# Moving the second tile's delta rule behind the first tile's expert choices, with fewer row buffers and panel slots lent twice

## The reference, cut to what matters

```python
h = _rmsnorm(x, norm1); proj = h @ w_in                    # split into 12 parts
o_a = _gated_delta_rule(q, k, v, beta, log_alpha)           # "delta": 64-token chunks in the reference
o_b = _hgrn2_recurrence(qb, 1 - f_gate, ib, log(f_gate))    # "hgrn"
mix = sigmoid(g_a) * (o_a @ w_branch_a) + sigmoid(g_b) * (o_b @ w_branch_b)
x = x + mix @ w_out
h2 = _rmsnorm(x, norm2)
# product keys: for 8 heads the top 16 of 128 x 128 keys, so 128 experts a token
s = einsum(h2 @ w_pq, sub_keys); idx, gate = top16(...)
y[t] = sum_k gate[t,k] * gelu(h2[t] . expert_u[idx[t,k]]) * expert_v[idx[t,k]]
```

## Time and profile before

| | us |
|---|---|
| median of 3 runs (1853.99 to 1854.33) | 1854.06 |
| the profiled execution, its own time | 1848.71 |
| its span, first to last instruction | 1846.9 |
| PE busy | 1614.6 (87%) |
| DVE busy | 993.5 (54%) |
| ACT busy | 461.3 (25%) |
| gathers, packets of queue q0 | 268.45 MB, 35.2% of 16 engines' span |
| HBM read | 469.04 MB, 255 GB/s over the span |

### The profile page before, as it was taken

One profiled execution on the slowest core, in us unless ns is written; L12 is line 12 of the kernel. 1 busy time (PEld: TensorE's weight loads), 2 busy tenths in 40 slices (PEclk: granted clock), 3 DMA queues, 4 the chain that ended last, 5 costly groups with the idle time before them and its releaser, 6 DMA issues.

```text
span 1846.9 us, 19442 instructions
## 1 busy us (share of the span) xinstructions
PE 1614.6 (87%) x7700; PEld 1076.7 (58%) x7700; DVE 993.5 (54%) x1843; ACT 461.3 (25%) x1018; POOL 312.2 (17%) x269
## 2 busy tenths in 40 slices
PE   7999989999897996989877667668999999899997
PEld 6857656764845553346423222227997486489963
DVE  3433334331676786358996666653666415356654
ACT  1152152240243554123323322221000013310001
POOL 0000000000112443233545545520000000000000
PEclk9999989999998998999988998899999999999999
DMA  6444221125799799999999999993644443155433
GB/s 243 175 157 168 86 92 46 48 101 209 315 424 369 311 422 419 425 422 419 421 420 421 422 421 421 422 392 126 223 166 154 183 160 137 46 205 183 174 146 114
DMA packets 55192, 471.32 MB, mean 255 GB/s; under 512 B 6592, under 2 KB 7744, under 8 KB 10432
## 3 DMA queue, kind: packets, MB, share of 16 engines
q0 software_dynamic: 36864, 268.45, 35.2%
q1 hardware_dynamic: 18240, 201.66, 28.8%
HBM read 469.04 MB, written 1.05 MB: 255 GB/s over the span
## 4 chain that ended last, share of the span: by engine, by line
PE 63%; DMA 17%; DVE 11%; ACT 4%; issue 3%; POOL 1%; SPq 0%; DVEq 0%; ACTq 0%; POOLq 0%
PE ps L2385 13%; DMA main<-in_expert_uv,main 10%; PE ps L489 7%; PE ps L445 6%; PE ps L1014 5%; PE ps L2542 5%; PE ps L415 5%; DMA panels<-in_expert_uv,main 4%; PE ps L1252 4%; DVE main L942 3%; PE ps L2312 3%; PE ps L2331 2%; PE ps L1486 2%; PE ps L485 2%; PE ps L2308 2%
## 5 line engine op out<-in xcount | busy, mean ns | idle before, releaser
L1014 PE MATMUL ps<-main 128*128 128x512 f32 x680 | 339.2, 648 | 95.6 <-ACT main L989 95.2
L924 POOL DMA_INDIRECT main<-in_expert_uv,main x208 | 246.8, 1187 | 377.5 <-PE ps L1014 225.7
L942 DVE SCALAR_TENSOR_TENSOR main<-main 128x1024 f32<-128x1024 f32 x208 | 249.5, 1223 | 93.2 <-DMA main<-in_expert_uv,main 92.0
L1014 PEld LDWEIGHTS ps<-main 128*128 128x128 f32 x680 | 134.5, 206 | 279.6 <-issue 145.9
L1014 PE MATMUL ps<-panels,main 128*128 128x512 f32 x148 | 81.7, 699 | 44.9 <-ACT main L989 37.2
L977 ACT ACTIVATE main<-main 128x2 f32<-128x2 f32 x128 | 25.9, 202 | 364.2 <-DVE main L942 299.2
L445 PE MATMUL ps<-panels,xT 128*128 128x512 f32 x256 | 112.5, 592 | 0.0
L2385 PE MATMUL ps<-main 128*128 128x128 f32 x912 | 104.9, 275 | 0.0
L2385 PEld LDWEIGHTS ps<-main 128*128 128x128 f32 x912 | 103.4, 192 | 0.0
L489 PE MATMUL ps<-panels,main 128*128 128x512 f32 x192 | 87.4, 615 | 4.9 <-ACT main L547 4.9
L1252 PEld LDWEIGHTS ps<-main 128*128 128x128 f32 x704 | 82.0, 192 | 11.9 <-issue 8.8
(11 more groups left out here) (320 smaller groups left out, 2367.3 us busy)
## 6 DMA issues: line engine op xcount, KB each, us to landing
panels<-in_wall SPq DMA_DIRECT2D x87, 2048.0 KB, 8.2
main<-in_rows SPq DMA_DIRECT2D x14, 512.0 KB, 8.9
main<-in_expert_uv,main POOLq DMA_INDIRECT x208, 20.8
main<-in_sub_keys SPq DMA_DIRECT2D x2, 1024.0 KB, 13.7
main<-in_wall SPq DMA_DIRECT2D x1, 2048.0 KB, 12.7
mats<-in_mats SPq DMA_DIRECT2D x1, 1088.0 KB, 5.2
x<-in_x SPq DMA_DIRECT2D x2, 512.0 KB, 4.2
main<-in_pool_w SPq DMA_DIRECT2D x1, 1024.0 KB, 32.7
```

The lines of the kernel that those rows point to most:

```text
L924: pool.indirect_dma_start(out=self.bufs[self.buf_of[r]], out_offset=None, in_=self.c.dram["expert_uv"], in_offset=bass.IndirectOffsetOnAxi ...
L942: dve.scalar_tensor_tensor(out=u, in0=u, scalar=1.0, in1=self.c.row(m, H2), op0=ALU.mult, op1=ALU.mult, accum_out=self.dots_at[:, m, q:q + ...
L1014: mm = pe.matmul(self.c.ps[:, b, :], self.diags[self.of_pe(r) % DIAG_RING], v[:, half * HALF:(half + 1) * HALF], start=(q == 1), stop=(q = ...
```

## The change: what it does

- The list of the order is rewritten. hgrn0 runs beside delta0 rather than beside delta1; tile 0's branches, mix, projection and choices follow at once; delta1 begins between them (its `norm` in front of tile 0's second branch) and its seven levels run beside the first choices and rows 0 to 31.
- hgrn0 gets six slots of its own (9 to 14 of the scratch area) in place of three of its own and three of tile 0's q, k and v. The states move to slots 15 and 16, the kept arrays to 17; `main` grows from 37 to 38 pieces of 1024 numbers a partition and the descriptor scratch of dynamic DMAs shrinks from 8192 to 4096.
- 15 row buffers in place of 18. Buffers open to a row: 4 for rows 0 to 8, 8 for 9 to 37, then 4 until row 42, 6 until 52, 10 until 66, 6 until 72, 9 until 105, 11 until 127, then 15. Before: 5 for rows 0 to 3, then 9, 6 (16 to 19), 10 (20 to 23), 13 (24 to 55), 9 (56 to 77), 11 until 127, then 15.
- The panel slots are lent to rows 9 to 37, taken back for tile 1's first six panels (SP now loads the first two of them anew, and so w_pq.0 no longer loads them ahead), lent to rows 53 to 66, and taken back for tile 1's branches.
- `ADDED` is a list of 64 rows (29 of them below 128) in place of every fourth row outside the choices (49, 17 below 128).
- Tile 1's choices stand at rows 126 to 139 of the list rather than at rows 93 to 128.
- In `tile`, the first branch's product no longer waits for the recurrence: `a` stands ahead of `turn_b`.

The diff, cut; the list of the order is shown where the text speaks of it:

```diff
-MAIN = 37 * D
+MAIN = 38 * D
-STATE_A, STATE_B, KEPT_IN = 12, 13, 14
+STATE_A, STATE_B, KEPT_IN = 15, 16, 17
...
-ADD_EVERY = 4
-CHOICES = ((1, 28), (92, SLOTS))
-ADDED = [r for r in range(0, 2 * SLOTS, ADD_EVERY) if not any(a <= r < b for a, b in CHOICES)]
+ADDED = [0, 13, 14, 25, 26, 28, 32, 37, 40, 44, 47, 49, 57, 64, 68, 77, 80, 83, 84, 87, 88, 89, 94, 97, 102,
...
-PANELS_FROM = 20
-PANELS_UNTIL = 56
-PARTS_FROM = 78
-CHOICE_FREE = 24
-DELTA_FREE = 4
-SCRATCH_UNTIL = 16
+PANELS_FROM = 9
+EARLY_AT = 38
+PANELS_AGAIN = 53
+PANELS_UNTIL = 67
+PARTS_FROM = 106
+CHOICE_FREE = 73
+DELTA_FREE = 43
...
-        in_scratch = [c.area(SCRATCH + UV * n, UV) for n in range(6)]
-        self.bufs = in_panels + in_tile0 + in_tile1 + in_scratch + [c.area(35 * D, UV)]
+        in_delta, in_hgrn = [c.area(SCRATCH + 6 * D, UV)], [c.area(SCRATCH + 9 * D + UV * n, UV) for n in range(3)]
+        self.bufs = in_panels + in_tile0 + in_tile1 + in_delta + in_hgrn
...
-            if r in (PANELS_FROM, SLOTS):
-                last = "b_q.1" if r == PANELS_FROM else "w_pq.1"
+            if r in (PANELS_FROM, PANELS_AGAIN, SLOTS):
+                last = {PANELS_FROM: "w_pq.0", PANELS_AGAIN: "b_q.1", SLOTS: "w_pq.1"}[r]
                 pool.wait_ge(self.c.panel_done.sem, FIRST[last] + COUNT[last])
-            if r == 0:
-                pool.wait_ge(*self.c.un.read_out("delta1.w"))
...
-        if m == 0:
-            slots = [slot(9), slot(10), slot(11)] + [c.part(0, a) for a in (Q_A, K_A, V_A)]
-        else:
-            slots = [slot(n) for n in range(6)]
+        slots = [slot(n) for n in (range(6) if m else range(9, 15))]
...
+        if m:
+            for r in c.experts.panel_slots[EARLY_AT]:
+                c.experts.wait_used(sp, r)
+            c.restart(sp, f"{EARLY[0]}.1")
...
+    part("tile0", "a", "turn_b")
+    part("delta1", "norm")
+    part("tile0", "b")
+    part("delta1", "turn")
+    part("tile0", "mix", "out", "norm")
+    part("delta1", "decay")
+    part("tile0", "pq0a", "scores0", "pq0b", "scores1", "top0")
+    part("delta1", "kk")
+    part("tile0", "best0", "name0", "pq1")
...
+    rows(35)
+    part("delta1", "o", "S")
+    rows(41)
+    part("beside1", 0)
...
+    rows(126)
+    part("tile1", "scores0", "pq0b", "scores1")
+    rows(128)
+    part("tile1", "top0", "best0", "name0", "pq1", "scores2", "top1", "best1", "name1", "pq2", "pq3", "scores3", "top2", "best2", "name2", "scores4")
+    rows(129)
+    part("tile1", "top3", "best3", "name3", "top4")
+    rows(131)
+    part("tile1", "best4")
+    rows(134)
+    part("finish", 0)
+    rows(135)
+    part("tile1", "name4")
...
-    nc = bacc.Bacc("TRN2", target_bir_lowering=False, num_devices=1, dynamic_dma_scratch_size=8192)
+    nc = bacc.Bacc("TRN2", target_bir_lowering=False, num_devices=1, dynamic_dma_scratch_size=4096)
```

More of the change, by code:

```diff
@@ L1873, in part, with rows @@
             order.append((of, stop))
-    def rows(n, most=SLOTS):
-        n = min(n, most - slots[0])
-        if n > 0:
-            slots[0] += n
-            order.append(("rows", slots[0]))
-    beside = [iter(range(len(BESIDE[m]))) for m in range(TILES)]
-    def panel(m, n=1):
-        for _ in range(n):
-            at = next(beside[m])
-            order.append((f"beside{m}", at))
-            order.append((f"read{m}", at))
-    panel(0)
+    def rows(n):
+        order.append(("rows", n))
@@ L1901, in mixers_order @@
+    part("read0", 5)
+    part("hgrn0", "k_t")
     part("delta0", "XY1")
-    panel(0)
-    for l in range(2, LEVELS):
-        part("delta0", f"P{l}")
-        panel(0)
-        part("delta0", f"XY{l}")
+    part("beside0", 6)
+    part("read0", 6)
+    part("hgrn0", "span0", "both0")
+    part("delta0", "P2")
+    part("beside0", 7)
+    part("read0", 7)
+    part("hgrn0", "a0", "pick0")
+    part("delta0", "XY2")
+    part("beside0", 8)
+    part("read0", 8)
+    part("hgrn0", "span1", "both1")
@@ L1907, in mixers_order @@
+    part("hgrn0", "a3", "pick3")
+    part("delta0", "XY5")
+    part("beside0", 14)
+    part("read0", 14)
+    part("hgrn0", "span4", "both4")
+    part("delta0", "P6")
+    part("beside0", 15)
+    part("read0", 15)
+    part("hgrn0", "a4", "pick4")
+    part("delta0", "XY6")
+    part("beside0", 16)
+    part("read0", 16)
+    part("hgrn0", "span5", "both5")
     part("delta0", "uw")
-    panel(0)
+    part("beside0", 17)
+    part("read0", 17)
+    part("hgrn0", "a5", "pick5")
     part("delta0", "ws", "o", "S")
-    at = next(beside[0])
@@ new lines, in mixers_order @@
+    part("tile0", "b")
[5 more added lines that the diff above has]
+    part("tile0", "best0", "name0", "pq1")
+    part("delta1", "P0", "XY0")
+    part("tile0", "scores2", "top1", "best1", "name1")
+    rows(1)
+    part("tile0", "pq2")
+    part("delta1", "P1")
+    part("tile0", "pq3", "scores3")
+    rows(5)
+    part("delta1", "XY1", "P2")
+    rows(9)
@@ L1956, in mixers_order @@
+    part("delta1", "XY2", "P3")
+    part("tile0", "top2")
+    part("delta1", "XY3")
+    rows(13)
+    part("tile0", "best2")
+    rows(15)
+    part("tile0", "name2", "scores4")
+    part("delta1", "P4")
+    rows(19)
+    part("delta1", "XY4")
+    rows(20)
+    part("delta1", "P5")
+    rows(26)
+    part("delta1", "XY5", "P6")
+    rows(27)
     part("delta1", "XY6")
+    rows(28)
     part("delta1", "uw")
-    part("tile0", "turn_b", "a")
+    rows(32)
     part("delta1", "ws")
-    part("tile0", "b", "mix", "out")
@@ L1961, in mixers_order @@
-    part("delta1", "o")
-    part("tile0", "norm")
-    part("delta1", "S")
-    part("tile0", "pq0a", "scores0", "pq0b", "scores1", "top0", "best0", "name0")
-    part("tile0", "pq1", "scores2", "top1")
-    part("delta1", "gate")
-    part("tile0", "best1", "name1")
-    part("tile0", "pq2", "pq3", "scores3")
-    rows(2)
-    part("beside1", 0)
-    part("tile0", "top2")
+    rows(35)
+    part("delta1", "o", "S")
+    rows(41)
+    part("beside1", 0)
+    part("tile0", "top3")
+    rows(42)
@@ L1988, in mixers_order @@
     part("tile0", "best3")
-    part("read1", 4)
-    rows(2)
+    rows(50)
     part("beside1", 5)
     part("tile0", "name3")
-    part("read1", 5)
-    part("tile0", "top4", "best4", "name4")
-    rows(4)
-    labels = ["k_t"] + [f"{x}{l}" for l in range(LEVELS) for x in ("span", "both", "a", "pick")]
-    for x in labels + ["ends"]:
-        part("hgrn1", x)
-        rows(1 if x[:-1] in ("span", "a") else 2)
-    part("hgrn1", "o")
-    rows(3)
-    part("hgrn1", "S")
-    rows(1)
+    rows(51)
@@ new lines, in mixers_order @@
+    part("read1", 4, 5)
+    part("hgrn1", "k_t", "span0")
+    part("tile0", "top4")
+    rows(53)
+    part("hgrn1", "both0")
+    rows(55)
+    part("hgrn1", "a0")
+    rows(58)
+    part("tile0", "best4")
+    part("hgrn1", "pick0", "span1", "both1")
+    rows(63)
+    part("tile0", "name4")
+    rows(65)
+    part("hgrn1", "a1", "pick1", "span2", "both2")
+    rows(66)
+    part("hgrn1", "a2")
+    rows(70)
+    part("hgrn1", "pick2", "span3", "both3")
+    rows(77)
+    part("hgrn1", "a3", "pick3", "span4", "both4", "a4")
@@ L2012, in mixers_order @@
     part("tile1", "b")
[L2013 removed]
+    rows(118)
     part("tile1", "mix")
[L2015 to L2033 removed]
@@ L2034, in mixers_order @@
[L2034 to L2050 removed]
+    rows(123)
@@ new lines, in mixers_order @@
+    part("tile1", "out", "norm", "pq0a")
+    rows(126)
[7 more added lines that the diff above has]
+    rows(134)
+    part("finish", 0)
+    rows(135)
+    part("tile1", "name4")
+    rows(139)
+    part("pool0", "rms")
@@ L2051, in mixers_order @@
+    rows(140)
+    part("pool0", "pooled")
+    rows(151)
+    part("pool0", "mixed")
+    rows(165)
+    part("pool0", "ln", "turn")
+    rows(259)
     part("finish", 1)
```

220 lines of the change are left out of this document (90 added, 130 removed).

## The result

The changed kernel takes **1869.12 us** (1868.29 to 1871.35, four runs) where the kernel before took 1854.03 beside it: a ratio of 1.0088, interval 1.007 to 1.0105. It is slower by 15 to 16 us. The forecast was 1836, range 1812 to 1866: wrong in sign, and outside its range. The profiled execution took 1868.43, 19.7 more than that of before.

The account below looks back on a forecast made before the run. PE was taken to bound the time to the first gather, the DMA engines the gathers, with an unchanged 600.7 after. The terms put the last landing at 1228, 18 earlier, so 1854 - 18 = 1836 us, range 1812 to 1866.

Parts of the forecast that it names:

- Term 1: Up to the first gather: less PE work and idle time puts that gather at 439, 46 earlier.
- Term 2: Rows 0 to 127: 458 us from the first scores, so row 127's dot ends at 877, 53 earlier.
- the head start survives this far: At row 127's dot: the first gather's lead of 46 is still there, the dot ending 53 before its old time.
- the part with the six panels: Rows 41 to 52: PE 66 at 92% busy plus 8 for the first panel, 74 in all.
- four-buffer round trips: Rows 4 and 8, whose gathers wait for rows 0 and 4: DVE waits some 7 and 10.
- Term 3: At row 128: its gather goes out 26 after row 127's dot, at 903, and the last landing is at 1228.
- The DMA engines starve in front of row 128: Slower rival, rows 53 to 127: DMA share 0.89, 28 more, time 1864; chance 0.22.
- Its sign: DMA share below 0.9 between rows 53 and 127 in the new profile would show the starving rival.
- Head start kept: Rival at row 128: the seam costs nothing, the whole 46 is kept, time 1808; chance 0.08.
- no difference: Rival in rows up to 40: they take 176 in place of 158, time 1854; chance 0.12.
- smaller descriptor scratch: Gathers in flight: half of 12, six, cover 15 us, more than the 5.8 an empty queue needs; cost 0.

Follow-up runs that it names:

- run 6: Run 1 with the panel slots taken back at row 33 instead of 38: 1876.09 us, ratio 1.0119 to the kernel before.
- run 3: The changed kernel with panel slots lent from row 4 instead of row 9: 1872.83 us, ratio 1.0117 to the kernel before.
- run 4: Run 1 with panel slots lent from row 4 instead of row 9: 1862.03 us, ratio 1.005 to the kernel before.
- run 2: The kernel before with tile 1's choices (all but the first two scores) put behind row 128 in the list: 1875.92 us, ratio 1.0127.
- run 7: The kernel before with hgrn0 beside delta0 in its own slots, delta1 ahead of the choices beside later projection pieces; 18 buffers: 1855.99 us, ratio 1.0015.
- run 1: The changed kernel with tile 1's branches and choices placed earlier in the list: 1857.33 us, ratio 1.0031 to the kernel before.
- run 11: Run 1 with 8 more rows in ADDED (105 to 116), sums moved from PE to DVE: 1862.76 us, ratio 1.0054 to the kernel before.
- run 13: Run 11 with the seven sums DVE had between rows 136 and 161 given to PE: 1857.5 us, ratio 1.0029 to the kernel before.
- run 12: Run 11 with rows 8, 17, 20 and 31 also in ADDED: 1862.09 us, ratio 1.0053 to the kernel before.
- run 14: Run 1 with only the seven sums DVE had between rows 136 and 161 given to PE: 1857.66 us, ratio 1.0025.

## Why the prediction was wrong, step by step

**Term 1** said 439 for the first gather; it is 446. From first scores to gather it said 20; in PE's timeline of the changed kernel the first scores stand at 425.7, which makes 20.3. Tile 0's norm waits 4.2 on DVE, as said (4).

```profile
415.14 1.97 PE L538 MATMUL ps<-mats,main 128*128 128x128 f32 x8 [4.16 <-DVE main L1752]
...
425.71 0.68 PE L1625 MATMUL ps<-main 128*128 128x128 f32 x4 [0.52 <-issue]
```

The 7 us lie ahead of the scores. The stretch up to the first scores, before and after:

```profile
0.00:474.40 474.40, 438.21 (x2152) 312.18 (x2152) 157.37 (x220) 128.42 (x146) 1.56 (x7) 0.98 0.37 137
```
```profile
0.00:425.70 425.70, 393.30 (x1756) 268.38 (x1757) 125.71 (x193) 121.01 (x138) 1.55 (x7) 0.98 0.42 153
```

PE's busy time falls by 44.9, where the sum of delta1's parts said 46.5; its idle time falls from 36.2 to 32.4, by 3.8, where the prediction took 9 as gained net. So the work removed was right, and the term mis-sized is that gain. It is a small miss: other traces with the same order up to there have the first gather at 442.

**Term 2 is the step that failed**, with its conclusion that row 127's dot ends 53 before its old time and "the head start survives this far". It ended 23.5 before. Counted from the first gather, the forecast had that dot after 438 us; it took 461.

| to the dot of row | said, from the first gather | measured |
|---|---|---|
| 40 | 138 | 143 |
| 52 | 212 | 225 |
| 72 | 267 | 277 |
| 107 | 354 | 371 |
| 127 | 438 | 461 |

The 23 us are made of five parts: 5 more to row 40, 8 more in the part with the six panels (82 instead of 74), 3 less in rows 53 to 72 (52 instead of 55), 7 more in rows 73 to 107 (94 instead of 87) and 6 more in rows 108 to 127 (90 instead of 84). The last three were made from the DMA engines' time alone: 2.48 a row with share 1.01 from 682 on. That rate was taken from a kernel with 9 buffers and full queues behind it. The changed one reaches row 53 with six buffers open and comes to it dry (0.84 over 200 us), and its DMA share is 0.92 between the gathers of rows 52 and 72 and 0.97 from there to row 107's; the three parts together took 10 more than said. That fewer open buffers cause this is an argument, which run 6 supports only in other rows. The other 13 lie ahead, in the two parts made from PE's time and some waits. In the part with the six panels PE waits 9.1 for a panel, near the 8 that was said, so the excess there has another cause, which no run shows:

```profile
593.95 9.70 PE L489 MATMUL ps<-panels,xT 128*128 128x512 f32 x16 [9.11 <-DMA panels<-in_wall]
```

The four-buffer round trips came near what was said: DVE waits 6.1 and 7.5 for a landing at rows 4 and 8 (said 7 and 10), and lending the panels earlier (runs 3 and 4) won nothing.

**Term 3, the seam, held:** a hole, row 128's gather 30 behind the dot (said 26), last landing 329 after that gather (said 325). Run 2 prices this part alone at 23.5.

One reading of the trace was also wrong: the earlier trace rows has a 7 in the fourteenth slice (600 to 646 us), so even before the DMA engines were not at 9 tenths throughout; the windows of the earlier trace rows that the sums use have it right.

The sum was 1228 for the last landing: 7 from term 1, 23 from term 2, 8 from term 3 make 1266.

**The rivals.** "The DMA engines starve in front of row 128" decides where that dot ends later than 895: it ended at 907, and the time is 1869 against its 1864. That its time comes so near is partly luck: it priced its place, rows 53 to 127, at 28 more, and these took 10 more; the rest came from term 1, from the rows ahead and from the seam. Its sign, DMA below 0.9 between rows 53 and 127, was not there but for the hole itself. Against it I had set that nine buffers ran at 1.01, in a stretch into which the DMA engines came full. "Head start kept" is out. So is "no difference": it put 18 more into the rows up to 40, which took 5 more.

**Where the head start went.** It is not a gain that was then lost by one mishap. Delta1's 46 us of PE work were not removed but put among rows 0 to 35, and the DMA engines' idle time in rows 0 to 51 doubled (20 to 41); the whole rise lies in rows 0 to 15. PE is not full there, so the sum of its work alone does not account for it; opening the ring earlier does not help either (run 3). Run 7, with delta1 in front and 18 buffers, keeps 22 idle in rows 0 to 51 and next to none behind them up to row 191. That delta1's steps among the first rows are the cause is the likely reading, but no run tests it alone. Then come the reload and fewer buffers (run 6 shows their weight: 16 us for five rows), then the seam. Filling the seam by order alone (run 1) returns 10.5; filling most of the rest (run 11) moves row 128's gather 23 earlier than in the changed kernel and returns nothing more, for DVE's choices now stand behind it.

**What stays open.** Runs 1, 11 and 13 idle 72 to 74 us in all. Of the pieces, only those at and behind the seam differ by more than equal programs do, and runs 11 to 14 show one cause there (DVE's work behind the seam); that it must add up to the same is not shown. Also open is what makes the 20 us in rows 0 to 15, delta1's work, the panels that moved away from there or the buffers: no run changed delta1's place alone with 15 buffers. The lead time of a gather with the smaller descriptor scratch showed nothing: the last gathers took 27 us to land as before; no run changed it alone.

Of the page cited ahead, the Trainium skill ("DMA: Bandwidth & Descriptors", the section on the anatomy of one DMA), whose fit gives 4.4 us for 1 MB: no gather in either trace lands that fast. The shortest was 5.8 before and is 8.9 in the changed kernel (its gathers, us from issue to landing):

```profile
DMA to landing us min/median/max: 8.9/20.7/30.2
```

## What to carry to other kernels

When a stretch is bound by the DMA engines, an earlier start is worth only what the engines can use: write down, row by row, their idle time in the new order (length less bytes over the full rate) before believing it, and treat a full-rate figure as valid only where the queue is full and as many buffers are open as in the rows it comes from. Work moved out of the critical front into a stretch that feeds DMA is not gone; ask of every such microsecond which engine there has it to spare. Where effects are of a few us, take two traces of the same program first: here equal stretches differed by 6. And a hole behind one wait is often the front of the next: two experiments, one that makes the hole in the old kernel and one that fills it in the new, tell its price from its worth.
